# The second block's attention units: ScalarE makes all copies out of PSUM

## The reference

```python
for layer in range(DEPTH_2):          # 2 layers
    x = x + mixers[layer](rms_norm(x, mix_norms[layer]))
    x = x + memory_cross_attention(rms_norm(x, xn), rms_norm(mem, mn), wq, wkv, wo)
    x = x + swiglu(rms_norm(x, fn), wg, wu, wd)
return rms_norm(x, final_norm)
```

```python
p = softmax(q @ k.T * scale + mask)
o = p @ v
```

## Time and profile before

| | |
|---|---|
| median of 3 runs (lowest, highest) | 4990.51 us (4985.95, 5001.51) |
| the profiled execution's own time | 4990.46 us |
| its span, first to last instruction | 4988.5 us |
| mean granted TensorE clock | 0.832 of full |
| TensorE matmuls busy | 4030.2 us (81%) |
| VectorE busy | 2167.9 us (43%) |
| ScalarE busy | 723.9 us (15%) |
| GpSimd busy | 1213.9 us (24%) |

### The profile page before, as it was taken

One profiled execution on the slowest core, in us unless ns is written; L12 is line 12 of the kernel. 1 busy time (PEld: TensorE's weight loads), 2 busy tenths in 40 slices (PEclk: granted clock), 3 DMA queues, 4 the chain that ended last, 5 costly groups with the idle time before them and its releaser, 6 DMA issues. The chain is left out here.

```text
span 4988.5 us, 44280 instructions
## 1 busy us (share of the span) xinstructions
PE 4030.2 (81%) x16708; PEld 2864.3 (57%) x16708; DVE 2167.9 (43%) x4531; ACT 723.9 (15%) x1672; POOL 1213.9 (24%) x1136
## 2 busy tenths in 40 slices
PE   7388978899873666666676799988997788999899
PEld 7155537877731223323244577665676556877687
DVE  6422134333338777675555554565543332023201
ACT  0122111111111111111112110122101221012100
POOL 0000002111104665464742344444441000000000
PEclk9698775555586888888897899998998888998899
DMA  8300110000016888787974699986895113431243
GB/s 223 57 26 22 46 53 1 1 1 1 1 48 209 316 314 291 271 312 263 377 281 134 220 343 356 322 275 221 315 354 185 50 46 98 152 117 60 68 144 110
DMA packets 476408, 833.52 MB, mean 167 GB/s; under 512 B 46819, under 2 KB 330910, under 8 KB 476190
## 3 DMA queue, kind: packets, MB, share of 16 engines
q0 software_dynamic: 147456, 536.94, 30.0%
q1 hardware_dynamic: 328742, 293.77, 19.0%
HBM read 828.44 MB, written 2.17 MB: 167 GB/s over the span
## 5 line engine op out<-in xcount | busy, mean ns | idle before, releaser
L2255 PE MATMUL banks<-arena 128*128 128x256 f32 (+1 forms) x4992 | 1143.6, 386 | 30.0 <-DVE arena L2325 27.4
L2255 PEld LDWEIGHTS banks<-arena 128*128 128x128 f32 (+1 forms) x4992 | 956.2, 193 | 231.7 <-issue 85.5
L1911 PE MATMUL banks<-arena 128*128 128x512 f32 x1280 | 712.6, 693 | 332.7 <-ACT arena L1929 220.0
L1844 POOL DMA_INDIRECT arena<-in_peer_v,arena x512 | 592.1, 1156 | 954.4 <-PE banks L1911 711.6
L1963 DVE CUSTOM_DVE_ANT_0 arena<-arena 128x1024 f32<-128x1024 f32 x512 | 628.5, 1228 | 289.4 <-DMA arena<-in_peer_u,arena 273.1
L1911 PEld LDWEIGHTS banks<-arena 128*128 128x128 f32 x1280 | 265.6, 219 | 674.8 <-issue 395.1
L1844 POOL DMA_INDIRECT arena<-in_peer_u,arena x512 | 533.0, 1041 | 406.9 <-DVE arena L1796 218.4
L517 PE MATMUL banks<-arena 128*128 128x512 f32 (+1 forms) x768 | 311.9, 565 | 2.3 <-DVEq L285 2.3
L3021 PE MATMUL banks<-arena 128*128 128x256 f32 x1408 | 313.0, 378 | 0.0
L3021 PEld LDWEIGHTS banks<-arena 128*128 128x128 f32 x1408 | 265.6, 189 | 47.7 <-issue 10.6
L3063 DVE TENSOR_TENSOR arena<-banks,arena 128x512 f32<-128x512 f32 x44 | 30.4, 692 | 602.0 <-PE banks L2255 602.0
(11 more groups left out here) (325 smaller groups left out, 4421.6 us busy)
## 6 DMA issues: line engine op xcount, KB each, us to landing
arena<-in_l_w_gate SPq DMA_DIRECT2D x44, 1024.0 KB, 6.5
arena<-in_l_w_up SPq DMA_DIRECT2D x44, 1024.0 KB, 6.6
arena<-in_l_w_down SPq DMA_DIRECT2D x44, 1024.0 KB, 6.1
arena<-in_ada_w SPq DMA_DIRECT2D x48, 512.0 KB, 7.2
arena<-in_l_w_qkv SPq DMA_DIRECT2D x24, 1024.0 KB, 6.0
arena<-in_w_in SPq DMA_DIRECT2D x36, 512.0 KB, 4.0
arena<-in_l_w_out SPq DMA_DIRECT2D x16, 1024.0 KB, 5.2
arena<-in_peer_q_w SPq DMA_DIRECT2D x16, 512.0 KB, 4.6
```

The lines of the kernel that those rows point to most:

```text
L1844: p.e.indirect_dma_start(e.ring[slot], None, tables[table], bass.IndirectOffsetOnAxis(ap=e.IDX[h][:, t, j:j + 1], axis=0)).then_inc(*p.up( ...
L1911: ins = p.e.matmul(k.bank[b], e.diag[x % 4], e.ring[slot][:, half * T:half * T + T], start=h == 0 and j == 0, stop=h == HEADS - 1 and j == ...
L2255: ins = p.e.matmul(out, left(c), right(c), start=c == 0, stop=c == c_n - 1, skip_group_check=True)
```

## The change

The copies out of bank 4 that VectorE made, for odd units and for tile 1, are now made by ScalarE with the instructions it used for the others. The two signals of VectorE (`dve_weights`, `dve_stored`) go, and whoever waited for them waits for ScalarE's. The order of steps stays as it is.

```diff
@@ stores_of
-            out.setdefault(x.block, []).append(((k.S.act_stored, k.S.dve_stored)[x.tile % 2], (name, u)))
+            out.setdefault(x.block, []).append((k.S.act_stored, (name, u)))
@@ units_pe
-            p.claim(("bank", 4), (S.act_weights, S.dve_weights)[u % 2], key)
+            p.claim(("bank", 4), S.act_weights, key)
...
-            p.wait_ge((S.act_weights, S.dve_weights)[u % 2], key)
+            p.wait_ge(S.act_weights, key)
...
-            p.claim(("bank", 4), (S.act_stored, S.dve_stored)[x.tile % 2], key)
+            p.claim(("bank", 4), S.act_stored, key)
@@ units_act
-        elif step == "weights" and u % 2 == 0:
+        elif step == "weights":
             if u >= 2:
                 p.wait_ge(S.output_filled, (name, u - 2))
             p.wait_ge(S.weights_filled, key)
-            p.e.activation(a.PT[0][:, 0:x.m], k.bank[4][:, 0:x.m], ACT.Copy).then_inc(*p.up(S.act_weights, key))
-        elif step == "store" and x.tile % 2 == 0:
+            p.e.activation(a.PT[u % 2][:, 0:x.m], k.bank[4][:, 0:x.m], ACT.Copy).then_inc(*p.up(S.act_weights, key))
+        elif step == "store":
@@ units_dve
-        elif step == "weights" and u % 2 == 1:
-            if u >= 2:
-                p.wait_ge(S.output_filled, (name, u - 2))
-            p.wait_ge(S.weights_filled, key)
-            p.e.tensor_copy(a.PT[1][:, 0:x.m], k.bank[4][:, 0:x.m]).then_inc(*p.up(S.dve_weights, key))
...
-        elif step == "store" and x.tile % 2 == 1:
-            p.wait_ge(S.store_filled, key)
-            p.e.tensor_copy(x.dst, k.bank[4][:, 0:P]).then_inc(*p.up(S.dve_stored, key))
```

## The result

| | before | after |
|---|---|---|
| median of 12 runs (lowest, highest), us | 4995.34 (4985.95, 5001.51) | 5006.25 (4996.98, 5014.20) |
| profiled execution: own time, span, us | 4990.46, 4988.5 | 5014.20, 5012.3 |
| ratio after to before, 95% interval | | 1.0024 (1.0015 to 1.0033) |

The change makes the kernel 0.24% slower, some 12 us by the ratio (the medians are 10.9 us apart); 5004 us (+0.27%) was forecast. The profiled execution of after is the longest of its twelve, and its span is 23.8 us above that of before. Of these, 13.6 lie ahead of the first unit's scale (2631.7 us before, 2645.3 after), in code that is the same; in the other profiles of this study the same point lies between 2629.6 and 2642.1, so this part goes with the execution. The eight unit runs give +13.3, all the rest -3.1.

A forecast was written before the change was run, and what follows sets the result against it. No engine is full in the unit runs; they go by latency where fill matmuls don't cover it. Terms 5.0 + 9.6 + 2.8 + 3.2 - 1.3 - 0.8 - 5.4 = +13.1 us give 5004 us, range 4979 to 5026.

The forecast's parts named there:

- Term 1: Unit runs: odd tiles' output copies, now behind ScalarE's exponential, delay the next transpose; 5.0 us cross, 9.6 us even and dilated.
- The cross pair: Sign in the cross loop: two units, 5.14 us before, take 5.60, in two halves of 2.80.
- Term 2: Unit runs: odd units' weight copies behind the exponential make the next transpose wait a copy longer, 7 x 0.4 = 2.8 us.
- Term 3: Beside the experts: ScalarE's diagonal matrices for expert matmuls stand behind waiting weight copies; 3.2 us taken, 6.5 at most.
- Term 4: VectorE relieved of copies: gains 1.3 us in cross runs, 0.8 in the last even run, 5.4 beside the experts.
- No gain from shorter copies: Copies moved to ScalarE: 43 ns less each at 128x256, at most some 5.5 us together; nothing counted.
- the even and dilated runs of half 1: Sign in runs of tokens 256 to 511: each grows by 2 to 4 us; the forecast is wrong if they don't grow.
- Hidden anyway: Rival: fill matmuls between output's and weights' transposes absorb the later copies, about nothing in sum, 4991 us; chance 0.17.
- VectorE paced the first half: Rival, tokens 0 to 255: all 21.7 us of copies come back, second half loses 7.2, 4976 us; chance 0.08.
- ScalarE's queue and the clock: Rival: all upper bounds, 5015 us, and one more cross run falling to 1.2 GHz, 5021 us; chance 0.20.
- The clock the other way: Rival: forecast losses, but the slow cross run and dilated tail go at full clock, 4983 to 4998 us; chance 0.10.
- The stretches outside the units: Sign: the forecast is wrong if feed-forward stretches, untouched by the change, move by more than the unit runs.

The follow-up runs named there:

- stores_only: Kernel before with only the output copies of odd tiles moved to ScalarE, weight copies left as they were; ratio 1.0051 to before, median 5024.05 us.
- weights_only: Kernel before with only the weight copies of odd units moved to ScalarE, output copies left as they were; ratio 1.0002 to before, median 4997.90 us.
- store_first: Changed kernel with ScalarE's output copy issued ahead of the next unit's exponential instead of behind it; ratio 0.9888 to before, median 4941.22 us.
- stores_dve: Kernel before with all output copies on VectorE, weight copies still shared; ratio 0.9924 to before, median 4957.95 us.
- warm_cross: Kernel before plus one unread matmul ahead of each exponential wait in the second half's cross runs, 16 in all; ratio 0.9969, median 4976.01 us.
- warm_before: Kernel before plus one unread matmul ahead of the exponential wait in all 80 units of tokens 256 to 511; ratio 0.9961, median 4977.90 us.
- warm_after: Changed kernel plus one unread matmul ahead of the exponential wait in all 80 units of tokens 256 to 511; ratio 1.0026 to before, median 5010.31 us.
- half0: Kernel before with the whole change only in units of tokens 0 to 255, beside the experts; ratio 1.0007 to before, median 4996.44 us.
- half1: Kernel before with the whole change only in units of tokens 256 to 511; ratio 1.0022 to before, median 5003.13 us.

## Why the prediction was right, and where it was not

**Term 1, the output copies (14.6 us)**, held in mechanism, place and size: +14.0 us idle in `stores_only`, minimum to transpose +0.78 us in the even run (0.81 forecast) and +0.55 in the last cross run (0.62 forecast: 0.78 before, 1.33 from 4723.62 to 4724.95 in after), 51 waits for L2575 (49 forecast). The cross pair takes 5.47 us, 5.60 forecast and 5.14 before.

**Terms 2 to 4** were +2.8, +3.2 and -7.5, in sum -1.5. `weights_only` has -0.2 idle and a ratio of 1.0002, so the sum is borne out. Its members are not.

Term 2 rests on a misreading of the earlier trace rows. The 14 waits for L2560 and L2567 are those of weight loads, and the transposes themselves waited for neither. At 4001.59 in before such a load has 0.81 us of idle time ahead of it, and its transposes start at 4001.60 with none. In `weights_only` they wait 25, 24 and 4 times for L2575, the VectorE output copy and L2564, as in before, and neither there nor in after does a weights' transpose wait for a weight copy (L2572). No run shows the 2.8 us. Waits of half 1's even run in before (us in total, times, longest us):

```profile
PE banks L2524 <- ACT arena L2575: 3.1, 3, 1.7
PE banks L2524 <- DVE arena L2632: 2.5, 3, 1.0
...
PEld banks L2524 <- ACT arena L2567: 1.6, 2, 0.8
```

Term 3: TensorE's waits for a diagonal (L1911 for L1929, 2600 to 4760 us) were 26 times and 24.0 us before, 28 and 25.6 in `weights_only`, 27 and 24.6 in after, so +1.6 and +0.6 where 3.2 was taken. Term 4's 5.4 us beside the experts are not seen: half 0's even and dilated runs have 1.6 us more idle time in `weights_only`, not less. Its cross runs, all four, have 1.9 less (1.3 forecast). That terms which were too large on both sides cancelled is luck. The weight copies' part is not quite independent of term 1 either: on top of the output copies the weight copies win 4.1 us of idle time back (14.0 to 9.9), 3.0 of it in the four cross runs, where term 4 counted 1.3, and 2.1 in half 0's dilated run, with small losses elsewhere.

**No gain from shorter copies.** In after's groups, 2600 to 4760 us, the weight copy keeps its 382 ns (381 in the earlier trace rows):

```profile
L2572 ACT ACTIVATE arena<-banks 128x256 f32<-128x256 f32 x80 | 30.5, 382 | 120.2 <-PE banks L2524 119.9
...
L2572 ACT ACTIVATE arena<-banks 128x128 f32<-128x128 f32 x32 | 8.8, 273 | 62.1 <-PE banks L2524 62.0
```

From 128 to 256 elements it grows by 109 ns, which leaves an estimated 164 for none. VectorE's has 289 and 424, so 135 and 154. By this the difference of 43 ns lies in the price per element, not in the fixed part. The Trainium skill, "Perfetto Trace Analysis", section "Optimizing Scalar/DVE Operations", puts the difference into the fixed part, some 125 ns of overhead on PSUM for VectorE and 51 for ScalarE. These rows do not show that.

**The sum.** +13.1 us was forecast; the unit runs of after are 13.3 longer, the ratio is worth 12. That the total agrees so well is in part luck. By idle time the change costs 9.9 us, 6.4 of it in half 1 (7.2 forecast) and 3.5 in half 0 (5.9 forecast). The other 3.4 are the balance of matmul times between +7.6 and -5.2 in single runs.

**What failed** is the step that treated the clock as two rivals, a misfortune in one direction or the other, at 0.20 and 0.10. It was no rival but a second term. It also broke what I said one would see, the even and dilated runs of half 1 longer by 2 to 4 us each, and by that sign alone the forecast would count as wrong: half 1's even run grew by 10.5 us and not 2 to 4, of which 3.0 are idle, and the dilated run shrank by 0.6 although its idle time grew by 2.6. Both idle figures are as forecast. I should have forecast idle time, and priced the clock beside it. The same gap made my expectations of `stores_only`, `store_first`, `stores_dve`, `warm_cross`, `warm_before` and `warm_after` wrong in size: they left the clock out or gave it too little.

**The rivals.** Hidden anyway (4991 us) falls with `stores_only`: the copies are not covered. VectorE paced the first half (4976) falls with `half0`. ScalarE's queue and the clock (5021) is close to what `stores_only` became, 5024, but not after. The clock the other way did take place in one run, -5.2 us in the first cross run of half 1, and was outweighed by the even run. The stretches outside the units, which I had named as a sign against the forecast, moved by 13.6 - 3.1 = 10.5 us in the profiled execution, less than the unit runs, and nearly all ahead of the first unit.

**Open.** Why `stores_only` is slower than the whole change. Of 14.6 us between them in the unit runs, 4.1 are idle and 10.5 matmul time. The same instructions of half 1 ran at another clock in `half1` and in after, so what comes ahead of a run has its part in it; what exactly decides which cross run falls to 1.2 GHz was not found. Nor was why the change gains matmul time once the output copies come first.

## What to carry to other kernels

Look at what stands ahead of a copy that empties a PSUM bank in its engine's in-order queue, not at how long the copy takes on which engine: moving 48 copies behind an exponential cost 14 us of idle time, and issuing them ahead of it (`store_first`) gave the fastest kernel of this study, 0.9888 of before (0.9885 with the 16 added matmuls, the same within noise). Where TensorE stands still between short steps, forecast its idle time from the chain of waits, and give the clock a term of its own: here it was from a third of the idle time's change (after) to twice it (`store_first`). Compare kernels by idle and busy time of each stretch, since the length alone mixes the two.

## What the hardware did that I had not expected

Idle gaps on TensorE were mostly paid for twice, and not at a fixed rate. In `stores_only` +14.0 us of idle time came with +13.9 us of slower matmuls, and in `store_first` -17.0 with -32.6, but in after +9.9 with only +3.4. The clock showed two levels, and a stretch of 43 us can run at the lower one although TensorE works in 38.07 of them. In before the last 52 us or so of that run are at 0.50, in `store_first` only the last 4.

Doing more can be faster: `warm_cross` adds 16 matmuls and saves 15.5 us. The Trainium skill, "TensorE: Matmul & The Clock Gate", part 1, has TensorE fall to 1.2 GHz after idleness. The direction agrees with `warm_cross`. What `warm_after` shows speaks against making much of it: its 80 added matmuls bought nothing over after (1.0026 and 1.0024), and the dilated tail stayed at 0.50. On the kernel before, the 64 of the 80 matmuls that lie outside the cross runs bought hardly anything either (0.9961 and 0.9969).
